# The front of a diffusion-transformer layer on one Trainium2 core: adaLN sections and first projection interleaved by pairs of k-tiles

## The reference, cut to what matters

```python
def _rms(x, g):
    return x * rsqrt(mean(x * x, axis=-1) + EPS) * g

mod_x = silu(c) @ ada_w + ada_b            # (6 * 1024): sh1, sc1, g1, sh2, sc2, g2
mod_c = silu(c_ctx) @ ada_w + ada_b
hc = _rms(ctx, norm1) * (1 + cc1) + ch1    # 256 context tokens
hx = _rms(x, norm1) * (1 + sc1) + sh1      # 1024 tokens of 1024 values
kvc = hc @ w_in[:, OFF_K:OFF_G]
zx = hx @ w_in                             # 4352 columns: Hyena 1536, q k v 768, gates 2048
filters = sin(fq * (sin(fq * (sin(fq * (feat @ fw1 + fb1)) @ fw2 + fb2)) @ fw3 + fb3)) @ fout
...                                        # Hyena convolution, attention, merge, 16 experts
```

## Time and profile before

| what | value |
|---|---|
| median of 3 runs | 2143.32 us (2141.97 to 2143.74) |
| profiled execution | 2140.15 us, its span 2138.4 us |
| PE busy | 2102.5 us, 98% |
| VectorE, ScalarE, GpSimd busy | 1680.3, 1177.3, 199.7 us |
| mean granted TensorE clock | 0.995 of full speed |

### The profile page before, as it was taken

The page is one execution under the profiler, slowest core; times in us unless marked ns, Lnnn a source line. Parts: engine busy times, 40 slices in busy tenths (PEclk is TensorE's granted clock), DMA queues, the critical chain, the costliest instruction groups (busy, mean ns, idle before and its releaser), DMA issues.

```text
span 2138.4 us, 28033 instructions
## 1 busy us (share of the span) xinstructions
PE 2102.5 (98%) x10357; PEld 1682.9 (79%) x10357; DVE 1680.3 (79%) x1829; ACT 1177.3 (55%) x1283; POOL 199.7 (9%) x86
## 2 busy tenths in 40 slices
PE   9999999989999999999999999999999999999998
PEld 4998888866678786787588888888888888888886
DVE  4667766158885998855888988889988988889986
ACT  4421222146622212334277777777777787877874
POOL 1000000000000001200020222012220222102200
PEclk9999999999999999999999999999999999999999
DMA  8135355240013126453899999999999999999993
GB/s 320 58 103 167 128 187 168 50 148 16 16 50 128 57 91 218 140 173 109 319 401 409 401 401 382 392 396 375 380 378 398 390 380 376 386 401 381 377 378 106
DMA packets 185388, 541.69 MB, mean 253 GB/s; under 512 B 16718, under 2 KB 59056, under 8 KB 184673
## 3 DMA queue, kind: packets, MB, share of 16 engines
q1 hardware_dynamic: 175256, 508.92, 63.1%
q0 software_dynamic: 5264, 17.00, 3.1%
q10 hardware_dynamic: 4792, 14.74, 1.9%
HBM read 504.97 MB, written 35.66 MB: 253 GB/s over the span
## 4 chain that ended last, share of the span: by engine, by line
PE 60%; DVE 1%; issue 0%; DMA 0%; POOL 0%; ACT 0%; POOLq 0%; DVEq 0%
PE p_y L340 5%; PE p_y L342 5%; PE p_y L341 5%; PE p_b L340 5%; PE p_b L341 5%; PE p_b L342 5%; PE p_a L342 5%; PE p_a L340 5%; PE p_a L341 5%; PE p_m L340 2%; PE p_m L341 2%; PE p_m L342 2%; PE p_t L2999 1%; PE p_a L3028 1%; PE p_m L2258 1%; PE p_t L2990 1%
## 5 line engine op out<-in xcount | busy, mean ns | idle before, releaser
L2866 DVE TENSOR_TENSOR r_lo<-ring,r_hi 128x2048 fp32r<-128x2048 f32 x372 | 839.0, 2287 | 58.8 <-ACT r_hi L2825 57.5
L2825 ACT ACTIVATE r_hi<-ring 128x2048 fp32r<-128x2048 f32 x372 | 708.6, 1916 | 148.5 <-PE p_b L342 76.3
L340 PE MATMUL p_y<-r_hi,a_hi 128*128 128x512 f32 x512 | 205.3, 401 | 0.0
L342 PE MATMUL p_y<-r_hi,a_lo 128*128 128x512 f32 x512 | 200.0, 391 | 0.0
L341 PE MATMUL p_y<-r_lo,a_hi 128*128 128x512 f32 x512 | 199.2, 389 | 0.0
L340 PE MATMUL p_b<-r_hi,x_hi 128*128 128x512 f32 x496 | 193.1, 389 | 0.0
L342 PE MATMUL p_b<-r_hi,x_lo 128*128 128x512 f32 x496 | 193.0, 389 | 0.0
L341 PE MATMUL p_b<-r_lo,x_hi 128*128 128x512 f32 x496 | 192.9, 389 | 0.0
L340 PE MATMUL p_a<-r_hi,x_hi 128*128 128x512 f32 x480 | 189.8, 395 | 0.0
L342 PE MATMUL p_a<-r_hi,x_lo 128*128 128x512 f32 x480 | 187.3, 390 | 0.0
L341 PE MATMUL p_a<-r_lo,x_hi 128*128 128x512 f32 x480 | 186.8, 389 | 0.0
(11 more groups left out here) (425 smaller groups left out, 3866.9 us busy)
## 6 DMA issues: line engine op xcount, KB each, us to landing
ring<-in_w_gate SPq DMA_DIRECT2D x128, 1024.0 KB, 10.5
ring<-in_w_up SPq DMA_DIRECT2D x128, 1024.0 KB, 9.3
ring<-in_w_down SPq DMA_DIRECT2D x128, 1024.0 KB, 12.4
w_raw<-in_w_in SPq DMA_DIRECT2D x17, 1024.0 KB, 6.4
ada_rest<-in_ada_w SPq DMA_DIRECT2D x16, 1024.0 KB, 5.4
ada<-in_ada_w SPq DMA_DIRECT2D x8, 1024.0 KB, 15.2
gate_dram<-zs ACTq DMA_DIRECT2D x16, 512.0 KB, 2.6
x_normed<-gate_dram SPq DMA_DIRECT2D x16, 512.0 KB, 4.2
```

The costliest lines, as they stand in the source:

```text
L340: pe.matmul(out, a_hi, b_hi, start=start, stop=False)
L342: return pe.matmul(out, a_lo, b_hi, start=False, stop=stop)
L2825: act.activation(r_hi[:, i % PARTS], ring[:, i % RAW], ACT.Copy).then_inc(hi_ready, 1)
L2866: dve.tensor_tensor(r_lo[:, i % PARTS], ring[:, i % RAW], r_hi[:, i % PARTS].bitcast(F32), ALU.subtract).then_inc(lo_ready, 1)
```

## The change

Units 0 and 1 become one product for tokens 0 to 511: the weight parts lie side by side in `w_parts`, and `first_tokens` multiplies with 512 moving columns, into four banks, so that `p_x` keeps two. A section is now 256 columns of shift and the 256 of scale that belong to the same two k-tiles; two buffers are used in turn. `sums` places k-tile k in the column group k % 4 of the array, with `sil` padded to 32 columns (`sil_wide`); the copy takes the whole bank, and `fold` adds the four groups by a matmul with `quarters` while turning them to columns. `modulation` follows for two k-tiles at a time, and the first tokens' work on these k-tiles runs between the sections. Tokens 0 to 511 are loaded first, section 3 ahead of the later tokens; sections 2 and 3 wait in SyncE's queue for a buffer. Squares and norms of tokens 512 to 1023 stand behind the first tokens' last k-tiles on ScalarE and VectorE. `late_tokens` does unit 0 for tiles 4 to 7 by k-tiles, then `project` unit 1. The filter layers come later. Some small tiles move to `g1row` and `g2row`, tokens 0 to 511 into `qkv`'s space. The last wait for scattered rows moves from GpSimd to SyncE.

```diff
-    EARLY = 8
-    groups = [(u, t, None) for u in range(2) for t in range(NT // 2)]
-    groups += [(u, t, None) for u in range(2) for t in range(NT // 2, NT)]
+    FIRST = NEAR_T
+    groups = [(0, t, None) for t in range(NEAR_T)]
+    groups += [(u, t, None) for u in range(2) for t in range(NEAR_T, NT)]
+    EARLY = len(groups)
     groups += [(2, t, None) for t in range(NTA)]
...
-return i % 3 if i < EARLY else (i - EARLY) % BANKS
+return i % NEAR_T if i < EARLY else (i - EARLY) % BANKS
...
-w_hi, w_lo = [sb("w_hi0", [P, KD, UW], F32R)], [sb("w_lo0", [P, KD, UW], F32R)]
+w_parts = sb("w_parts", [P, 2, 2, KD, UW], F32R)
+w_hi, w_lo = ([w_parts[:, u, part] for u in range(2)] for part in range(2))
...
-x = sb("x_in", [P, NTA, D])
+x_late = sb("x_in", [P, NTA - NEAR_T, D])
...
+x_near = spare[:, NTA * QKV - NEAR_T * D:].rearrange("p (t d) -> p t d", d=D)
+x = [x_near[:, t] for t in range(NEAR_T)] + [x_late[:, t] for t in range(NTA - NEAR_T)]
...
+mod_rows = g["g1row"][:].rearrange("p (b n) -> p b n", b=2)
...
@@ -481,36 +489,41 @@
         sp.dma_start(rows1[64:72, :], A["c"].rearrange("o (j p) -> (o j) p", p=P)).then_inc(c_in, 16)
         sp.dma_start(rows1[72:80, :], A["c_ctx"].rearrange("(j p) -> j p", p=P)).then_inc(c_in, 16)
 
-        def load_section(i, half):
-            rows = slice(D // 2 * half, D // 2 * half + D // 2)
-            src = A["ada_w"][0][rows, 512 * i:512 * i + 512].rearrange("(k p) n -> p k n", p=P)
-            sp.dma_start(ada[:, i, KD // 2 * half:KD // 2 * half + KD // 2], src).then_inc(ada_in[2 * i + half], 16)
+        def load_section(i):
+            if i >= 2:
+                sp.wait_ge(section_done, i - 1)
+            for half in range(2):
+                rows = slice(D // 2 * half, D // 2 * half + D // 2)
+                for part in range(2):
+                    at = D * part + UW * i
+                    src = A["ada_w"][0][rows, at:at + UW].rearrange("(k p) n -> p k n", p=P)
+                    sp.dma_start(ada[i % 2][:, KD // 2 * half:KD // 2 * half + KD // 2, UW * part:UW * part + UW],
+                                 src).then_inc(ada_in[2 * i + half], 16)
 
         def load_x(i):
             src = A["x"][0, 2 * P * i:2 * P * i + 2 * P, :] if 2 * i < NT else A["ctx"][0]
-            sp.dma_start(x[:, 2 * i:2 * i + 2, :], src.rearrange("(t p) d -> p t d", p=P)).then_inc(x_in[i], 16)
-
-        for i in range(SECTIONS - 1):
-            load_section(i, 0)
-            load_section(i, 1)
-        load_x(0)
-        load_x(1)
-        load_section(SECTIONS - 1, 0)
-        load_section(SECTIONS - 1, 1)
+            dst = x_near[:, 2 * i:2 * i + 2, :] if 2 * i < NEAR_T else x_late[:, 2 * i - NEAR_T:2 * i - NEAR_T + 2, :]
+            sp.dma_start(dst, src.rearrange("(t p) d -> p t d", p=P)).then_inc(x_in[i], 16)
 
         def load(u):
-            if u == 2:
-                sp.wait_ge(w_lo_first, KD // 2)
-            elif u > 2:
-                sp.wait_ge(w_lo_ready, u - 2)
+            if 2 <= u < 4:
+                sp.wait_ge(w_lo_first[u - 2], KD // 2)
+            elif u >= 4:
+                sp.wait_ge(w_lo_ready, u - 3)
             c = unit_column(u)
             sp.dma_start(w[:, u % 2], A["w_in"][0][:, c:c + UW].rearrange("(k p) n -> p k n", p=P))\
               .then_inc(w_in[u % 2], 16)
+        load_x(0)
+        load_x(1)
+        load_section(0)
         load(0)
+        load(1)
+        load_section(1)
+        load_section(2)
+        load_section(3)
         load_x(2)
         load_x(3)
         load_x(4)
-        load(1)
         load(2)
         sp.wait_ge(lo_ready, len(GROUPS))
         sp.dma_start(nsink[:].rearrange("p k j -> p (k j)"), A["attn_sink"][0, :].partition_broadcast(P))\
...
-        pool.memset(spare[0:H2, L:L + 2 * H2], 0.0).then_inc(f_zero, 1)
-        pool.memset(spare[0:H2, 6144:6144 + 2 * H2], 0.0).then_inc(f_zero, 1)
+        pool.memset(g["g2row"][:, 0:KD * QUARTER], 0.0).then_inc(wide_zero, 1)
+        pool.memset(w1_all, 0.0).then_inc(f_zero, 1)
...
+        def first_high(u, q):
+            act.wait_ge(w_in[u], 16)
+            k = slice(2 * q, 2 * q + 2)
+            act.activation(w_hi[u][:, k], w[:, u, k], ACT.Copy).then_inc(w_hi_first[u], 1)
...
+            if i < FIRST:
+                act.activation(qkv[:, c, 0:2 * UW], src, ACT.Copy).then_inc(evacuated, 1)
...
+                else:
+                    act.wait_ge(sin_ready, 3)
...
+        for t in range(NEAR_T):
             square(t)
         roots(0, NEAR_T, 1)
-        high_part(0)
-        square(NEAR_T)
-        square(NEAR_T + 1)
-        act.wait_ge(mod_ready, 4)
-        for i, (h, k) in enumerate(GROUPS):
-            a, n = tokens(h)
+        first_high(0, 0)
+        for i in range(0, KD, 2):
+            modulate_act(i + 1)
+            high_tokens(i)
+            high_tokens(i + 1)
+            if i == 0:
+                first_high(0, 1)
+                first_high(1, 0)
+                first_high(1, 1)
+                for q in (2, 3):
+                    first_high(0, q)
+                    first_high(1, q)
+        for t in range(NEAR_T, NT):
+            square(t)
+        roots(NEAR_T, NT, 7)
+        for i in range(KD, len(GROUPS)):
+            if i == 2 * KD:
+                for n in range(FIRST, FIRST + 4):
+                    evacuate(n)
+                high_part(2)
...
+                modulate_act(i)
+            high_tokens(i)
+            if i == KD:
+                for n in range(FIRST):
                     evacuate(n)
-            if i in (9, 11):
-                square(NT + (i == 11))
-            if i == 13:
+            if i in (KD + 2, KD + 4):
+                square(NT + (i == KD + 4))
+            if i == KD + 5:
                 roots(NT, NTA, 13)
-            if i >= 9 and i % 2 and (i - 3) // 2 < EARLY:
-                evacuate((i - 3) // 2)
+            if i > 2 * KD and i % 2:
+                evacuate(FIRST + 4 + (i - 2 * KD) // 2)
+        sine(0)
...
+        dve.wait_ge(sil_ready, 1)
+        dve.wait_ge(wide_zero, 1)
+        dve.tensor_copy(sil_wide[:, :, 0:2].rearrange("p k v -> p v k"), sil[:]).then_inc(wide_ready, 1)
+        dve.wait_ge(consts, 3)
+        dve.tensor_reduce(quarters, ident[:].rearrange("p (j n) -> p n j", j=4)[:, 0:2], AX, ALU.add)\
+           .then_inc(quarters_ready, 1)
...
+            dve.tensor_copy(mod_rows[:, s_ % 2], p_sec[:]).then_inc(section_copied, 1)
+
+        def modulation(s_):
+            k = slice(2 * s_, 2 * s_ + 2)
+            sums = p_mod[:, 0:4 * KD].rearrange("p (a k v) -> p a k v", a=2, v=2)[:, :, k]
+            parts = mod[:, 0:2 * KD, :].rearrange("p (a k) v -> p a k v", a=2)[:, :, k]
+            bias = cols1[:, 0:2 * KD].rearrange("p (a k) -> p a k", a=2)[:, :, k]
+            dve.wait_ge(mod_t, s_ + 1)
+            dve.tensor_tensor(parts, sums, bias.unsqueeze(3).broadcast_to([P, 2, 2, 2]), ALU.add)\
+               .then_inc(mod_ready, 1)
+            dve.wait_ge(mod_ready, 2 * s_ + 1)
+            dve.scalar_tensor_tensor(out=scale[:, k, :], in0=parts[:, 1], scalar=1.0,
+                                     in1=cols1[:, 48 + 2 * s_:50 + 2 * s_].unsqueeze(2).broadcast_to([P, 2, 2]),
+                                     op0=ALU.add, op1=ALU.mult).then_inc(mod_ready, 1)
...
-        copy_section(0)
-        copy_section(1)
-        dve.wait_ge(f_in, 16 * 15)
-        filter_layer(0)
-        copy_section(2)
...
+        for i in range(0, KD, 2):
+            copy_section(i // 2)
+            if i == 2:
+                first_low(0, 2)
+            modulation(i // 2)
+            modulate(i)
+            if i == 0:
+                first_low(0, 0)
+            low_part(i)
+            low_part(i + 1)
+            if i == 0:
+                first_low(1, 0)
+                first_low(0, 1)
+                first_low(1, 1)
+            if i == 2:
+                first_low(1, 2)
+                first_low(0, 3)
+                first_low(1, 3)
+        mean_squares(NEAR_T, NT)
+        token_roots(NEAR_T, NT, 7, 2)
+        norm_tokens(NEAR_T, NT)
+        for i in range(KD, len(GROUPS)):
+            if i % 2 == 0 and i != 2 * KD:
                 modulate(i)
-            if i:
+            if i > KD:
                 low_part(i - 1)
-            if i == KD:
-                token_roots(NEAR_T, NT, 7, 2)
-                norm_tokens(NEAR_T, NT)
-                weights_low(1)
+            if i == 2 * KD:
                 modulate(i)
-            if i in (2, 4):
-                first_low(1 + i // 2)
-            if i == 6:
-                mean_squares(NEAR_T, NT)
-            if i == 13:
+            if i == KD + 5:
                 mean_squares(NT, NTA)
-            if i == 14:
+            if i == KD + 7:
                 token_roots(NT, NTA, 13, 3)
                 norm_tokens(NT, NTA)
+            if i == 2 * KD + 3:
+                weights_low(2)
         low_part(len(GROUPS) - 1)
-        filter_layer(1)
+        filter_layer(0)
...
```

(117 more changed lines are left out.)

147 lines of the change are left out of this document (48 added, 99 removed).

## The result

The changed kernel is **slower: 2150.32 us** in the median of 6 runs (2149.85 to 2150.62) against 2142.64 in 6 runs of the kernel before (2140.65 to 2145.05). The ratio is 1.004, with a 95% interval from 1.003 to 1.005. The forecast was 2144.8 with a range up to 2149.5, so the time lies outside it. The profiled execution has a span of 2148.4 us (before 2138.4), PE busy 2090.9 us (97%) in place of 2102.5 (98%), and a mean granted clock of 0.991 in place of 0.995. PE is busy 11.6 us less and the kernel takes 10 us longer.

The account below looks back on a forecast made before the run. PE, busy 98% of 2138.4 us, was taken as the bound. First product at 31.4, 94.1 us of work and 6.4 of waits put the projection at 131.9 against 130.4, +1.5: median 2144.8, range 2139.3 to 2149.5.

Parts of the forecast that it names:

- The frame: Whole kernel: the shift of the first Hyena projection's start, 130.41 before, is the shift of the end.
- a packed section: adaLN sections on PE: 16 passes in four column groups take 2.0 us instead of 7.03, bounds 1.8 and 7.0.
- the drain that was weighed: PE at tiling-mode changes around sections: eight drains of some 0.2 us would add 1.6 us; left out of the sum.
- first product: First product of the projection on PE, at 43.61 before: starts at 31.4, 12.2 us earlier.
- Rival A: Sections on PE: packing fails in part, each costs 4.0 instead of 2.0 us; +8, so 2152.8; unpacked 2165; chance 0.11.
- B: PE's thin stretch from 66 to 73 us: the clock falls again, costing 3.2 us, so 2148.0; chance 0.11.
- C: Front: late waits halved (2.2 less), clock up at 19 (2.9), perfect packing (0.8); projection at 126.0, 2138.9; chance 0.18.
- Waits behind it: PE from the first product at 31.4 to the projection: 94.1 us of work and 6.4 of waits, ending at 131.9.
- ten groups of unit 2: PE from 100.3: these products 28.8, filter layers 1.1, a sine wait 0.9, column sums 0.8, ending at 131.9.
- the sign of being wrong: Front: wrong if sections land later than PE comes to them, or waits behind the first product differ much from 6.4 us.
- Unit 3's low weights: VectorE before the projection: done at 129.5 to 131.5; without the 13.19 us idle as cover, 0 to 1.5 us more.
- The last wait: Kernel's end: moving the wait for scattered rows from GpSimd to SyncE was priced at nought, 0.5 either way.

Follow-up runs that it names:

- the repaired kernel: Changed kernel with unit 3's load issued right behind unit 2's and VectorE forming unit 3's low weights ahead of the third filter layer: 2141.3 us (0.9999).

## Why the prediction was wrong, step by step

**What held.** The frame: the start of the first Hyena projection does set the end. It moved by 10.04 us. The last scatter moved by 11.4, which is this shift and 1.6 more at the barrier, less 0.3 over the rest, where the low clock lies at other places in the two traces. The span moved by 10.0, as the wait on SyncE gives 1.4 back. PE's own terms held as well: a packed section at 1.86 us against 2.0, and products of 512 columns at once behind it, without the drain that was weighed with the Trainium skill, "TensorEngine Tiling (Array Packing)", section "Key Properties". The row above shows a spacing of 35.36 - 33.50 = 1.86 us from the section's first pass to the next product, and four by four the passes alone are 1.76 by the 0.44 of the earlier trace rows, which leaves at most 0.1 us for any drain. Normed tokens at 18.9 (19.1), first product at 30.16 (31.4), norms waited for until 66.68 (67.8), first late product at 69.67 (70.7). The first product was early because the clock rose within section 0, which took 3.17 us and not 4.0, and because the fold was at full speed. Rival A (packing fails) fell, and so did B: the granted clock is 1.00 from 60 to 80. Of C the packing came true, and a part of the clock.

**What failed** is "Waits behind it", and in it the sentence from "ten groups of unit 2" to "131.9". The sum gave this stretch a single wait of 0.9 us for a sine; from the first product to the projection it had 6.4 us of waits, and they came to 11.9, which the prediction itself had named as the sign of being wrong. The change puts the end of the token work later (84.92 to 101.30), and SyncE's queue has everything that follows behind that wait: the adaLN part, ten copies, and the load of unit 3. The prediction listed that SyncE's waits for sections 2 and 3 hold back the later tokens, and never asked the same of the `lo_ready` wait, which the change doesn't touch and only moves. The trace of before had what was needed: ScalarE had the weights 21.7 us behind the release, and the prediction's own sum has the release near 100.3, so the load at 122. Unit 2's evacuations begin near 101, and ScalarE has `high_part(3)` ahead of them. The stop could be read off before any run.

**What came out by luck.** With the two links taken out the sum is nearly met: the repaired kernel starts its projection at 131.20, against 131.9. In part that is luck, since three errors cancel. The window of the repaired kernel from the first product to the projection reads:

```profile
30.13:131.20 101.07, 96.62 (x684) 83.26 (x685) 52.38 (x103) 40.76 (x76) 0.00 (x0) 1.00 0.41 135
```

The first product came 1.3 us earlier than 31.4, the waits are 4.45 us and not 6.4, and PE is busy for 96.6 us and not 94.1.

**What was mis-sized.** "Unit 3's low weights would be done at 129.5 to 131.5, just at the edge; without that cover 0 to 1.5 us more" named the second link, but assumed the load to be in. They were done at 137.05 in the changed kernel:

```profile
126.31 0.35 DVE L892 TENSOR_SCALAR ada_acc<-ada_rest,sil 128x256 f32<-128x256 f32 x1 [11.97 <-DMA ada_rest<-in_ada_w]
134.77 2.28 DVE L767 TENSOR_TENSOR w_parts<-w_raw,w_parts 128x2048 fp32r<-128x2048 f32 x1
```

Even with the load early they ended at 134.66 and cost 2.06 of waiting and 1.7 at the low clock (0.79 in the window from 130 to 138), 3.8 us together. Up to the first attention product behind the front the two traces with and without this link differ by 5.1 (452.27 and 447.19), as the medians do; the other 1.3 was there at the first late product (70.97 for 69.66). The pause of 13.19 us on VectorE was taken as cover for work that moved; it lay behind the arrival of the adaLN part, not ahead of it, and the new kernel's VectorE has its 11.97 us pause at the wrong end, before that part. **The last wait**, put at nought with 0.5 either way, is worth -1.4: outside its bounds, and in the good direction. The sum had neither the stop from 118 to 126 nor the low clock behind it, which added 1.8.

In numbers: forecast of the shift +1.5; less 0.7, what is left of the three errors above; plus 7.46 waited and 1.8 of low clock; makes +10.0. The median is 5.5 above the forecast and not 8.5. The wait on SyncE takes 1.4 of the rest. The remaining 1.6 would lie in the reference, though that is worked out and not measured: the forecast added to a median of 3 runs, 2143.32, where later medians of the same kernel over 21 to 27 runs were 2141.5 to 2141.9.

**What stays open** is what decides where in an execution the clock gives way behind the barrier. The runs show only that it isn't the kernel alone. Whether fillers in the pause at the barrier would hold the clock was not tried. Nor was it shown how much of the 7.46 us would go if only the ten copies were moved in the changed kernel: they were moved only where the load already stood ahead of them.

## What to carry to other kernels

When a stage is moved later, list everything that is queued behind the semaphore on which it ends, on every queue, DMA issue above all, and recompute when each of these is there. The edit didn't touch the lines of that wait, the copies and the load behind it, and 7.46 us of waiting came from there. Put a load that needs only a free buffer ahead of every wait that it doesn't need. A pause on an engine is cover only if what ends it comes before the work that is to be hidden. And a wait removed shows the next link: follow the chain to the projection before the first one is priced.
